# Conditioned encoder layer: the order of first loads and of first work, tiles of x against blocks of conditioning weights

## The chip, the core and the metric

The kernel runs on one core of a Trainium2 chip. The core has five engines with an instruction list each: TensorE (PE, matmuls; its weight loads are shown as PEld), VectorE (DVE), ScalarE (ACT), GpSimd (POOL) and SyncE (SP), which here only issues DMAs. Engines wait for one another by semaphores. The metric is the device time of one execution in microseconds (us).

## What is computed

One layer with a SwiGLU block, attention and a second SwiGLU block, each behind a normalisation that is scaled and shifted by a conditioning vector, on 1024 + 512 tokens of width 1024, in float32:

```python
def trunk(x, c):
    mod = jax.nn.silu(c) @ ada_w[l] + ada_b[l]          # (1024) x (1024, 9 * 1024)
    sh1, sc1, g1, sh2, sc2, g2, sh3, sc3, g3 = jnp.split(mod, N_MOD, axis=-1)
    h = modulate(rmsnorm(x, ffn1_norm[l]), sh1, sc1)    # h * (1 + scale) + shift
    x = x + 0.5 * g1[:, None, :] * swiglu(h, ffn1_wg[l], ffn1_wu[l], ffn1_wd[l])
    h = modulate(rmsnorm(x, mix_norm[l]), sh2, sc2)
    x = x + g2[:, None, :] * token_mixing(h, w_in[l], ...)
    h = modulate(rmsnorm(x, ffn2_norm[l]), sh3, sc3)
    x = x + 0.5 * g3[:, None, :] * swiglu(h, ffn2_wg[l], ffn2_wu[l], ffn2_wd[l])
    return rmsnorm(x, final_norm[l])
```

The first product needs x, turned so that its width lies along the partitions, the reciprocal root of each token's mean square, and the first two of the nine parts of `mod` (sh1 and sc1), which are the first 2048 columns of `ada_w`.

## The kernel before

All is in one program, `build`, in which each engine's list is written out: `start_loads` and `ffn_loads` for SP, `start_pe`, `start_act` and `start_dve` for the start, and then the first SwiGLU block (`ffn_*`), attention and the second SwiGLU block. The change touches the start, and in it the following.

**Tiles of x.** x has twelve tiles (`NT`) of 128 tokens and 512 KB each, four (`TPC`) to a chunk. They are loaded (L660) into `x_in`, a ring of four places; a place is loaded again when PE has transposed its tile (`x_turned`) and ACT has squared it (`x_summed`). For each tile ACT sums the squares (L767), PE makes eight transposes into PSUM (L671), and then DVE copies one half to `XT` (L853) and ACT the other (L770). Two pairs of PSUM banks take turns (`x_kept_v`, `x_kept_s`). After each chunk ACT takes a root (L774) and DVE makes reciprocals and four diagonal matrices (L859, L864), with which PE spreads the reciprocals over the partitions (L684) for ACT to copy (L780).

**Conditioning blocks.** `ada_w` comes in blocks of 512 columns, 2 MB each (L648). The first four, 0 to 3, give sh1 and sc1. ACT makes the high half of each weight (L800, four pieces for a block, into the ring `ada_hi`), DVE the low half (L806, four pieces), and PE multiplies the conditioning by both, 16 matmuls for a block (L714, L716, L719). ACT copies the result's row (`ada_keep`, L791) and PE turns it (`ada_turn`, L731). Blocks 4 and 5, for the gate, are multiplied as they are (L706, 32 matmul records).

**Order.** SP issues all twelve tiles of x and then the blocks, all in one queue. PE, ACT and DVE do the three chunks of x first, with the spreading in between, and then block after block. `ffn_loads` goes on with block 4, waits for the last tile of x to be transposed and squared, and loads the first weight quarters (`quart`, L2274), with block 5 among them.

**First product.** Behind the blocks DVE forms `mod` (L892, L896), multiplies x by its reciprocal roots (L2181, four times), and forms sums and low halves of the operands (L2209, L2221); ACT shifts and scales (L2192) and makes high halves (L2217). ACT and POOL make high and low halves of the weight units (L2383, L2389), and POOL sums of quarters (L2411). PE's products (L2852 to L2854, 24 matmuls each) take one unit and one operand after the other.

**Memory.** `ada_w_sb` fills the front of a region of which `HW` bytes per partition are used so. `x_in` lies directly behind it, where `ada_hi` lies afterwards, so that no high half can be made while x is there. `quart` lies 24576 bytes further on.

Of the kernel before, what the change touches and what calls it, by code (L numbers as in the profile page):

```python
# [13 lines left out]
F32 = mybir.dt.float32  # L14
# [6 lines left out]
P = 128  # L21
# [56 lines left out]
def build(nc, io):  # L78

    with ExitStack() as ctx:  # L80
# [39 lines left out]
        s1 = ExitStack()  # L120
        XR = 4
        x_in = sb(s1, "x_in", [P, XR, D])
        s1.close()
# [43 lines left out]
        rstd_p, rows = placed(HW + 57344, [("rstd_p", [P, 2, NB], F32), ("rows", [P, P], F32)])  # L167
        x_junk, diag = placed(HW + 40960, [("x_junk", [P, 2, D], F32), ("diag", [P, 2 * TPC, P], F32)])
# [218 lines left out]
        xt_parked, PARK0 = rows_landed, 16 * len(row_plan)  # L387
# [258 lines left out]
        def ada_block_load(sp, b):  # L646
            half, c = ada_home(b)
            sp.dma_start(ada_w_sb[:, half, :, c, :], ada_src[:, :, b * CH:(b + 1) * CH]).then_inc(ada_landed[b], 16)  # L648

        def start_loads(sp):  # L650
            sp.wait_ge(consts_set, 1)
            for src, r0, nr, w in row_plan:
                sp.dma_start(rows[r0:r0 + nr, 0:w], src).then_inc(rows_landed, 16)
            sp.dma_start(ident[:, :], io["ident"]).then_inc(consts_landed, 16)
            for t in range(NT):
                x, r = (io["x_prompt"], t * P) if t < S_PROMPT // P else (io["x_sample"], t * P - S_PROMPT)
                if t >= XR:
                    sp.wait_ge(x_turned, 2 + t - XR + 1)
                    sp.wait_ge(x_summed, t - XR + 1)
                sp.dma_start(x_in[:, t % XR, :], x[0, r:r + P, :]).then_inc(x_landed[t % XR], 16)  # L660
            for b in range(4):
                ada_block_load(sp, b)
# [73 lines left out]
        def start_pe(pe):  # L736
            pe.sem_inc(x_turned, 2)
            pe.sem_inc(sq_used, 2)
            pe.wait_ge(rows_landed, 16 * len(row_plan))
            pe.wait_ge(consts_landed, 16)  # L740
            pe.transpose(PS[:, 4, 0:NROW], rows[0:NROW, :], ident[0:NROW, 0:NROW]).then_inc(par_psum, 1)
            x_turn(pe, 0)
            x_turn(pe, 1)
            spread_pe(pe, 0)
            spread_pe(pe, 1)
            x_turn(pe, 2)
            pe.wait_ge(silu_ready, 2)
            ada_block(pe, 0)
            ada_block(pe, 1)
            ada_turn(pe, 0)  # L750
            for b in range(2, 6):
                ada_block(pe, b)
                if b < 4:
                    ada_turn(pe, b - 1)
                if b == 3:
                    ada_turn(pe, b)
            spread_pe(pe, 2)
            spread_pe(pe, 3)
            ada_turn(pe, 4)
            ada_turn(pe, 5)  # L760
# [32 lines left out]
        def ada_split_hi(act, b, p):  # L793
            half, c = ada_home(b)
            if p == 0:
                act.wait_ge(ada_landed[b], 16)
            if 4 * b + p >= AH // 2:
                act.wait_ge(ada_used, 4 * b + p + 1 - AH // 2)
# [10 lines left out]
        def start_act(act):  # L809
# [9 lines left out]
            x_sums(act, 0)  # L819
            x_sums(act, 1)  # L820
            spread_act(act, 0)
            spread_act(act, 1)
            x_sums(act, 2)
            for b in range(4):
                ada_split_hi(act, b, 0)
# [40 lines left out]
        def start_dve(dve):  # L866
# [12 lines left out]
            x_keep_dve(dve, 0)  # L879
            spread_dve(dve, 0)  # L880
            x_keep_dve(dve, 1)
            spread_dve(dve, 1)
            x_keep_dve(dve, 2)
            spread_dve(dve, 2)
            for b in range(4):
                for p in range(KD // 2):
# [2192 lines left out]
```

## Time and profile before

| | us |
|---|---|
| median of 3 runs | 2986.58 |
| lowest, highest | 2986.42, 2987.47 |
| profiled execution, its own time | 2986.62 |
| its span in the profile | 2984.8 |
| PE busy in the span | 2869.9 |
| POOL busy | 2231.1 |
| DVE busy | 1742.5 |
| ACT busy | 1553.8 |

The profile is of one execution. The busy share says how long an engine had an instruction in work; where an engine's row ends in square brackets, it had stood idle for so long before it, and the name behind the arrow is what released it. The granted clock of PE is given as a share of full speed. A timeline row that covers several instructions is marked x2, x8 and so on, and its length goes from the first one's start to the last one's end. Windows sum up a stretch of the execution.

### The profile page before, as it was taken

Reading aid. Unit: us, or ns where it says so; the run is one execution under the profiler, and the core shown is the slowest. Engines: PE = TensorE matmul, PEld = TensorE weight load, DVE = VectorE, ACT = ScalarE, POOL = GpSimd, SP = SyncE. Lnnn points to the kernel's source line nnn. Section 1 sums busy time; section 2 is a strip of 40 time slices with the busy share of each in tenths; the row PEclk is TensorE's granted clock in tenths of the full one; section 3 lists DMA queues with packets and bytes.
Section 4 is the critical chain, followed back from the end, with each engine's and each line's share of the span. In section 5 each row is a group of like instructions: output and inputs, shape, how many; then the busy total and the mean of one; then the engine's idle time right before and its main releaser. Section 6 shows DMA issues by size and latency. Waiting matters only on the chain. (4 is left out here: it accounts for less than half of the span.)

```text
span 2984.8 us, 49320 instructions
## 1 busy us (share of the span) xinstructions
PE 2869.9 (96%) x16057; PEld 2643.6 (89%) x16057; DVE 1742.5 (58%) x3002; ACT 1553.8 (52%) x2585; POOL 2231.1 (75%) x1116
## 2 busy tenths in 40 slices
PE   6899999999999999997999999999999999999998
PEld 3899999999999988885666667989999999999998
DVE  5666777767777657876543332274544467544545
ACT  6534444544444467766767775453444355444444
POOL 0788888889888853234557666678898888889884
PEclk9999999999999999998999999999999999999999
DMA  8333233333433335556322235441222232122224
GB/s 283 104 97 117 90 114 100 109 129 99 127 96 116 120 138 146 140 157 153 103 58 77 73 96 158 115 127 57 86 63 77 76 122 99 57 85 63 77 73 160
DMA packets 378610, 323.46 MB, mean 108 GB/s; under 512 B 22780, under 2 KB 325743, under 8 KB 378479
## 3 DMA queue, kind: packets, MB, share of 16 engines
q1 hardware_dynamic: 375342, 320.21, 35.4%
q10 hardware_dynamic: 3136, 1.57, 0.2%
q8 instruction: 74, 1.21, 0.2%
q14 instruction: 58, 0.47, 0.1%
HBM read 263.29 MB, written 58.43 MB: 108 GB/s over the span
## 5 line engine op out<-in xcount | busy, mean ns | idle before, releaser
L2389 POOL TENSOR_TENSOR W_lo<-quart,W_hi 128x1024 fp32r<-128x1024 f32 x384 | 941.8, 2471 | 178.4 <-ACT W_hi L2383 178.1
L2852 PE MATMUL PS<-SL,W_hi 128*128 128x384 f32 x2112 | 715.6, 339 | 31.7 <-issue 16.5
L2854 PE MATMUL PS<-SL,W_lo 128*128 128x384 f32 x2112 | 709.8, 336 | 0.0
L2853 PE MATMUL PS<-SL,W_hi 128*128 128x384 f32 x2112 | 709.7, 336 | 0.0
L2383 ACT ACTIVATE W_hi<-quart 128x1024 fp32r<-128x1024 f32 x384 | 402.9, 1060 | 561.8 <-PE PS L2918 245.0
L2054 DVE SCALAR_TENSOR_TENSOR XT<-PS,mod,XT 128x384 f32<-128x384 f32 (+1 forms) x840 | 418.4, 527 | 271.9 <-PE PS L2918 169.5
L2852 PEld LDWEIGHTS PS<-SL,W_hi 128*128 128x128 f32 x2112 | 399.3, 189 | 40.3 <-issue 24.0
L1844 POOL TENSOR_TENSOR XT_r<-XT,XT_r 128x512 fp32r<-128x512 f32 x224 | 286.9, 1286 | 179.0 <-ACT XT_r L1696 178.6
L2853 PEld LDWEIGHTS PS<-SL,W_hi 128*128 128x128 f32 x2112 | 399.3, 189 | 1.0 <-issue 1.0
L2854 PEld LDWEIGHTS PS<-SL,W_lo 128*128 128x128 f32 x2112 | 399.0, 189 | 0.0
L2411 POOL TENSOR_TENSOR quart<-quart 128x1024 f32<-128x1024 f32 x128 | 317.2, 2478 | 10.4 <-DVE qsum L2411 1.2
L2496 ACT ACTIVATE SLf<-PS 128x384 f32<-128x384 f32 x264 | 129.0, 491 | 290.0 <-PE PS L2854 289.9
L2684 DVE TENSOR_TENSOR PS<-PS,SLf 128x384 f32<-128x384 f32 x176 | 96.3, 562 | 236.4 <-ACT SLf L2496 224.2
L2411 POOL TENSOR_TENSOR qsum<-quart 128x1024 f32<-128x1024 f32 x63 | 151.1, 2398 | 105.0 <-DMA quart<-in_ffn_wu 75.2
L2918 PE MATMUL PS<-XT_r,W_lo 128*128 128x384 f32 x640 | 214.1, 334 | 0.0
L2917 PE MATMUL PS<-XT_r,W_hi 128*128 128x384 f32 x640 | 214.1, 334 | 0.0
L2916 PE MATMUL PS<-XT_r,W_hi 128*128 128x384 f32 x640 | 214.1, 334 | 0.0
L1752 DVE TENSOR_REDUCE mbuf<-PS 128x1 f32<-128x1024 f32 (+1 forms) x96 | 100.5, 1047 | 146.4 <-PE PS L1552 146.4
L1690 ACT ACTIVATE XT<-PS 128x512 f32<-128x512 f32 x224 | 133.1, 594 | 92.9 <-PE PS L1588 67.9
L2389 POOL TENSOR_TENSOR W_lo<-qsum,W_hi 128x1024 fp32r<-128x1024 f32 x64 | 159.8, 2496 | 4.2 <-ACT W_hi L2383 4.0
L2916 PE MATMUL PS<-hid,W_hi 128*128 128x384 f32 x480 | 160.8, 335 | 0.0
L2917 PE MATMUL PS<-hid,W_hi 128*128 128x384 f32 x480 | 160.5, 334 | 0.0
(314 smaller groups left out, 6385.9 us busy)
## 6 DMA issues: line engine op xcount, KB each, us to landing
quart<-in_ffn_wg SPq DMA_DIRECT2D x176, 256.0 KB, 3.1
quart<-in_ffn_wu SPq DMA_DIRECT2D x176, 256.0 KB, 3.4
quart<-in_ffn_wd SPq DMA_DIRECT2D x160, 256.0 KB, 3.0
ada_r<-in_ada_w SPq DMA_DIRECT2D x128, 192.0 KB, 2.5
raw<-in_w_out SPq DMA_DIRECT2D x30, 512.0 KB, 3.9
ada_w_sb<-in_ada_w SPq DMA_DIRECT2D x6, 2048.0 KB, 19.2
XT<-scr_xt SPq DMA_DIRECT2D x8, 1536.0 KB, 8.6
scr_xt<-XT SPq DMA_DIRECT2D x4, 2688.0 KB
```

The source lines that it names most:

```text
L1690: act.activation(e_slot(i), PS[:, 2 + i % 2, :], ACT.Exp).then_inc(exps_done, 1)
L1844: pool.tensor_tensor(p_lo(i), e_slot(i), p_hi(i).bitcast(F32), ALU.subtract).then_inc(p_lo_done, 1)
L2054: mm = dve.scalar_tensor_tensor(out=xt, in0=PS[:, bank, a - c * NB:b - c * NB], scalar=hgate[:, g, m, s:s + 1], in1=xt, op0=ALU.mult, op1= ...
L2383: act.activation(W_hi[:, slot_of(S, u), :], unit_src(u), ACT.Copy).then_inc(unit_hi, 1)
L2389: pool.tensor_tensor(W_lo[:, slot_of(S, u), :], unit_src(u), W_hi[:, slot_of(S, u), :].bitcast(F32), ALU.subtract) \
L2411: eng.tensor_tensor(flat(out), flat(a), flat(b), op).then_inc(sum_ready, 1)
L2852: pe.matmul(out, w_hi, m_hi, start=j in PRODUCT_OPENS and kp == 0, stop=False, skip_group_check=True)
L2853: pe.matmul(out, w_hi, m_lo, start=False, stop=False, skip_group_check=True)
L2854: mm = pe.matmul(out, w_lo, m_hi, start=False, stop=kp == 3, skip_group_check=True)
L2916: pe.matmul(out, w_hi, m_hi, start=n in PRODUCT_OPENS and kt == 0, stop=False, skip_group_check=True)
L2917: pe.matmul(out, w_hi, m_lo, start=False, stop=False, skip_group_check=True)
L2918: mm = pe.matmul(out, w_lo, m_hi, start=False, stop=kt == 1, skip_group_check=True)
```

## The change

`x_in` is placed where `quart` lies later. SP issues four tiles of x and block 0, four tiles and block 1, four tiles and block 2, and then block 3, in two DMAs of 1 MB with a semaphore each; ACT waits for the second ahead of its third piece. PE, ACT and DVE follow this order: ACT makes the high halves of block b behind the tiles of chunk b, DVE likewise the low halves, and PE multiplies block 0 ahead of chunk 1's transposes, and block 1 ahead of chunk 2's. No instruction of ACT, DVE or PE is added or taken away.

```diff
-        s1 = ExitStack()
         XR = 4
-        x_in = sb(s1, "x_in", [P, XR, D])
-        s1.close()
...
+        x_in, = placed(HW + 24576, [("x_in", [P, XR, D], F32)])
...
         def ada_block_load(sp, b):
             half, c = ada_home(b)
+            if b == 3:
+                for k, landed in ((0, ada_landed[3]), (KD // 2, ada_tail)):
+                    sp.dma_start(ada_w_sb[:, half, k:k + KD // 2, c, :], ada_src[:, k:k + KD // 2, b * CH:(b + 1) * CH])                       .then_inc(landed, 16)
+                return
...
-            for t in range(NT):
-                x, r = (io["x_prompt"], t * P) if t < S_PROMPT // P else (io["x_sample"], t * P - S_PROMPT)
-                if t >= XR:
-                    sp.wait_ge(x_turned, 2 + t - XR + 1)
-                    sp.wait_ge(x_summed, t - XR + 1)
-                sp.dma_start(x_in[:, t % XR, :], x[0, r:r + P, :]).then_inc(x_landed[t % XR], 16)
-            for b in range(4):
-                ada_block_load(sp, b)
+            for c in range(NCH):
+                for t in range(c * TPC, (c + 1) * TPC):
+                    x, r = (io["x_prompt"], t * P) if t < S_PROMPT // P else (io["x_sample"], t * P - S_PROMPT)
+                    if t >= XR:
+                        sp.wait_ge(x_turned, 2 + t - XR + 1)
+                        sp.wait_ge(x_summed, t - XR + 1)
+                    sp.dma_start(x_in[:, t % XR, :], x[0, r:r + P, :]).then_inc(x_landed[t % XR], 16)
+                ada_block_load(sp, c)
+            ada_block_load(sp, 3)
...
             x_turn(pe, 0)
+            pe.wait_ge(silu_ready, 2)
+            ada_block(pe, 0)
             x_turn(pe, 1)
             spread_pe(pe, 0)
             spread_pe(pe, 1)
-            x_turn(pe, 2)
-            pe.wait_ge(silu_ready, 2)
-            ada_block(pe, 0)
             ada_block(pe, 1)
             ada_turn(pe, 0)
+            x_turn(pe, 2)
...
+            if b == 3 and p == 2:
+                act.wait_ge(ada_tail, TAIL0 + 16)
...
-            x_sums(act, 0)
-            x_sums(act, 1)
-            spread_act(act, 0)
-            spread_act(act, 1)
-            x_sums(act, 2)
             for b in range(4):
+                if b < NCH:
+                    x_sums(act, b)
+                if b == 1:
+                    spread_act(act, 0)
+                    spread_act(act, 1)
                 ada_split_hi(act, b, 0)
                 ada_split_hi(act, b, 1)
...
-            x_keep_dve(dve, 0)
-            spread_dve(dve, 0)
-            x_keep_dve(dve, 1)
-            spread_dve(dve, 1)
-            x_keep_dve(dve, 2)
-            spread_dve(dve, 2)
             for b in range(4):
+                if b < NCH:
+                    x_keep_dve(dve, b)
+                    spread_dve(dve, b)
                 for p in range(KD // 2):
                     ada_split_lo(dve, b, p)
```

PE's list at its beginning, before: the transposes of x (from `x_in`), the spreading (`diag`), and then the matmuls of block 0 (`ada_hi`, `ada_w_r`).

```order
L741 MATMUL PS<-ident,rows 128x117
L671 MATMUL PS<-ident,x_in 128x128 x64
L684 MATMUL PS<-diag,ones 128x128 x6
L671 MATMUL PS<-ident,x_in 128x128 x32
L716 MATMUL PS<-ada_hi,c_hl 4x512
L719 MATMUL PS<-ada_w_r,c_hl 2x512
L714 MATMUL PS<-ada_w_r,c_hl 2x512
```

PE's list in the changed kernel, from the end of block 0 to the beginning of block 1. Line numbers are 4 higher here.

```order
L718 MATMUL PS<-ada_w_r,c_hl 2x512
L720 MATMUL PS<-ada_hi,c_hl 4x512
L675 MATMUL PS<-ident,x_in 128x128 x32
L688 MATMUL PS<-diag,ones 128x128 x6
L720 MATMUL PS<-ada_hi,c_hl 4x512
L723 MATMUL PS<-ada_w_r,c_hl 2x512
L718 MATMUL PS<-ada_w_r,c_hl 2x512
```

The 32 transposes of chunk 1 now stand between block 0 and the spreading, and block 1 behind that. The turn of the first row (`ada_row`) and the transposes of chunk 2 stand between block 1 and block 2:

```order
L718 MATMUL PS<-ada_w_r,c_hl 2x512
L720 MATMUL PS<-ada_hi,c_hl 4x512
L735 MATMUL PS<-fold,ada_row 128x2 x4
L675 MATMUL PS<-ident,x_in 128x128 x32
L720 MATMUL PS<-ada_hi,c_hl 4x512
L723 MATMUL PS<-ada_w_r,c_hl 2x512
L718 MATMUL PS<-ada_w_r,c_hl 2x512
```

ACT's list before, from the last tile of x over the last root to the high halves (L800) and the copies of rows (L791):

```order
L767 ACTIVATE x_junk,x_stat<-x_in 128x1024
L770 ACTIVATE XT<-PS 128x4x128
L774 ACTIVATE x_stat<-x_stat,eps_col 128x4
L800 ACTIVATE ada_hi<-ada_w_sb 128x1024 x6
L791 ACTIVATE ada_row<-PS 4x512
L800 ACTIVATE ada_hi<-ada_w_sb 128x1024 x4
L791 ACTIVATE ada_row<-PS 4x512
```

ACT's list in the changed kernel, from tile 7's copy to tile 8's:

```order
L774 ACTIVATE XT<-PS 128x4x128
L778 ACTIVATE x_stat<-x_stat,eps_col 128x4
L784 ACTIVATE rstd_p<-PS 128x384 x2
L806 ACTIVATE ada_hi<-ada_w_sb 128x1024 x2
L795 ACTIVATE ada_row<-PS 4x512
L806 ACTIVATE ada_hi<-ada_w_sb 128x1024 x2
L771 ACTIVATE x_junk,x_stat<-x_in 128x1024
L774 ACTIVATE XT<-PS 128x4x128
```

Block 1's four high halves and the copy of block 0's row stand between the chunks, where tile 8 followed the spreading's copies directly.

## Rows read from the trace of the kernel before

**Rows 1.** Page, part 1: busy us (share of span) and instructions, by engine
```profile
PE 2869.9 (96%) x16057; PEld 2643.6 (89%) x16057; DVE 1742.5 (58%) x3002; ACT 1553.8 (52%) x2585; POOL 2231.1 (75%) x1116
```

**Rows 2.** Windows: from:to length, busy us (count) of PE, PEld, DVE, ACT, POOL; clock, DMA
```profile
0.00:62.40 62.40, 38.08 (x207) 22.29 (x208) 30.73 (x51) 41.90 (x66) 0.94 (x5) 0.92 0.87 312
...
107.00:300.00 193.00, 191.65 (x1107) 189.40 (x1107) 123.39 (x229) 82.24 (x129) 167.83 (x71) 0.99 0.39 120
```

**Rows 3.** Windows of the start: PE clock, DMA share and GB/s stand last
```profile
7.00:14.00 7.00, 4.91 (x25) 4.19 (x25) 1.81 (x6) 4.23 (x9) 0.00 (x0) 1.00 0.95 354
...
14.00:21.00 7.00, 4.34 (x32) 3.42 (x32) 3.63 (x9) 6.97 (x14) 0.00 (x0) 1.00 0.77 266
...
21.00:28.00 7.00, 4.42 (x36) 4.02 (x36) 3.67 (x9) 6.04 (x14) 0.00 (x0) 1.00 0.82 260
...
36.50:42.00 5.50, 2.94 (x8) 0.86 (x8) 4.32 (x4) 3.89 (x4) 0.00 (x0) 0.50 1.04 387
```

**Rows 4.** Timeline, tiles of x: start us, length us, engine, line, operation, idle before
```profile
14.14 1.09 PE L671 MATMUL PS<-ident,x_in 128*128 128x128 f32 x8 [0.18 <-DMA x_in<-in_x_prompt]
...
22.08 0.59 ACT L770 ACTIVATE XT<-PS 128x512 f32<-128x512 f32 x1
...
23.59 0.59 ACT L770 ACTIVATE XT<-PS 128x512 f32<-128x512 f32 x1
...
24.07 0.30 ACT L774 ACTIVATE x_stat<-x_stat,eps_col 128x4 f32<-128x4 f32 x1
...
24.62 0.88 DVE L864 TENSOR_SCALAR diag<-ident,x_stat 128x128 f32<-128x128 f32 x4
...
26.10 1.05 ACT L767 ACTIVATE x_junk<-x_in 128x1024 f32<-128x1024 f32 x1
```

**Rows 5.** Timeline, last tile of x and first conditioning block
```profile
29.73 1.09 PE L671 MATMUL PS<-ident,x_in 128*128 128x128 f32 x8 [0.51 <-DMA x_in<-in_x_sample]
...
36.60 3.89 ACT L800 ACTIVATE ada_hi<-ada_w_sb 128x1024 fp32r<-128x1024 f32 x4 [4.12 <-DMA ada_w_sb<-in_ada_w]
...
37.69 4.63 DVE L806 TENSOR_TENSOR ada_w_r<-ada_w_sb,ada_hi 128x1024 fp32r<-128x1024 f32 x4 [4.08 <-ACT ada_hi L800]
...
39.06 0.58 PE L716 MATMUL PS<-ada_hi,c_hl 128*4 128x512 f32 x1 [8.23 <-DVE ada_w_r L806]
...
44.31 0.62 PE L716 MATMUL PS<-ada_hi,c_hl 128*4 128x512 f32 x2
```

**Rows 6.** Timeline, later conditioning blocks on PE, ACT and DVE
```profile
49.42 0.40 PE L716 MATMUL PS<-ada_hi,c_hl 128*4 128x512 f32 x1
...
50.73 0.40 PE L716 MATMUL PS<-ada_hi,c_hl 128*4 128x512 f32 x1
...
54.96 0.59 ACT L791 ACTIVATE ada_row<-PS 4x512 f32<-4x512 f32 x1
...
55.45 1.99 ACT L800 ACTIVATE ada_hi<-ada_w_sb 128x1024 fp32r<-128x1024 f32 x2
...
56.53 2.36 DVE L806 TENSOR_TENSOR ada_w_r<-ada_w_sb,ada_hi 128x1024 fp32r<-128x1024 f32 x2 [0.21 <-ACT ada_hi L800]
```

**Rows 7.** Timeline, operand preparation and first products on DVE, POOL and PE
```profile
64.23 6.76 DVE L2181 TENSOR_TENSOR SLf<-XT,rstd_p 128x1536 f32<-128x1536 f32 x4
...
70.83 2.40 POOL L2411 TENSOR_TENSOR qsum<-quart 128x1024 f32<-128x1024 f32 x1 [6.81 <-DMA quart<-in_ffn_wu]
...
71.02 3.82 DVE L2209 TENSOR_TENSOR SLf<-SLf 128x1536 f32<-128x1536 f32 x1
...
90.30 0.66 PE L2852 MATMUL PS<-SL,W_hi 128*128 128x384 f32 x1 [7.06 <-issue]
...
91.79 1.75 DVE L2209 TENSOR_TENSOR SLf<-SLf 128x1536 f32<-128x1536 f32 x1
...
107.01 0.45 PE L2852 MATMUL PS<-SL,W_hi 128*128 128x384 f32 x1 [2.18 <-POOL W_lo L2389]
...
108.41 0.52 PE L2852 MATMUL PS<-SL,W_hi 128*128 128x384 f32 x1
```

More of the change, by code:

```diff
@@ L386, in build @@
         raw_kept, RAW0, t_made, MADE0 = diag_ready, NT, x_inv, NCH
-        xt_parked, PARK0 = rows_landed, 16 * len(row_plan)
+        ada_tail, TAIL0 = rows_landed, 16 * len(row_plan)
+        xt_parked, PARK0 = rows_landed, TAIL0 + 16
         xt_unparked, BACK0 = [consts_landed, ada_landed[5]], 16
```

## The prediction

> **What bounds the kernel now.** I read the page's busy shares first, then the windows of the start against a stretch of the body, then the timeline of the first 110 us, engine by engine. TensorE is busy for 2869.9 of 2984.8 us [rows 1]. In the body nothing is left to win: 191.65 of 193.00 us busy between 107 and 300 us. The start is different: 38.08 of the first 62.40 us, most of it transposes and thin matmuls that wait for data [rows 2]. The change edits the start alone. All its waits are relative (a semaphore of another engine), nothing later stands at a fixed time, and the body is bound by PE, so what the start gains or loses reaches the end undiminished. The question is when DVE has done its last low half of a conditioning block (57.7 to 58.89 in the profiled run) [rows 6], for the modulation, the operands of the first product and its matmuls follow from that.
>
> Two things hold up the start now. While x is loaded, the DMA engines move 260 to 266 GB/s, against 387 afterwards [rows 3], because the ring of four tiles is refilled only as ACT and PE release it. Then ACT stands for 4.12 us before block 0, 6.9 us after the last tile of x had landed (29.7 to 36.6), and DVE and PE for as long [rows 5]. From there the blocks come in every 5.4 us, as fast as the queue moves 2.1 MB at 387 GB/s, and the engines follow them.
>
> **The transfers.** The change fills the holes in the queue: 14 us at about 263 instead of 387 GB/s are 14 x (1 - 263/387) = 4.5 us of transfer time. With block 0 behind four tiles, the queue has moved 2.48 MB by 14 us [rows 3] (some 0.15 before 7 us), and tiles, rows and block 0 are 4.3 MB, so its data are over at 14 + 1.7/0.387 = 18.4 us. Bounds of the landing: tile 3 landed at 14.14 [rows 4], plus 5.4 us of one block, 19.5; or plus the 6.9 us that block 0 took behind the last tile before [rows 5], 21.0. I take 20.3, in the middle, ACT beginning at 20.4. After that no data are late: tiles 4 to 7 and block 1 are 4.2 MB, 10.8 us, down at about 31; tiles 8 to 11 are released until 34 and are down by 39, block 3 some 11 us later; each is wanted later than that, as follows. The new half loads of block 3 and the wait on their second half (ACT, before its third piece) therefore cost nothing; uncovered, they would cost at most a half block, 2.7 us. The ring's new place costs nothing either: SP already waited for all tiles before it loaded the first weight quarter, though this wait now ends at about 51 us, with the queue still busy on block 4.
>
> **The engines.** Each engine runs its list in order, and the lists are now woven: four tiles, one block. The work is the same, instruction for instruction. What is new is who stands behind whom: the copies of tile 4 on ACT wait for PE's transposes, which stand behind block 0's 16 matmuls, which wait for DVE's low halves, which wait for ACT's high halves. This round trip through four engines comes twice more. I lay it out with offsets from rows.
>
> Block 0. ACT begins at 20.4. In the trace the first matmul came 2.46 us after ACT's begin (36.60, 39.06), and the next thing on PE could start 7.94 us after it (the second matmul of the row at 44.31 starts at 44.54) [rows 5]. PE was at half clock for the first 3.9 us of these (0.50 granted between 36.5 and 42.0 [rows 3]), after standing 8.23 us; in the new order it stands from 15.2 to 22.9, as long, so I keep the offset. Tile 4's transposes start at 28.3 and its copy on ACT at 29.4. ACT had finished the four high halves at 24.4 and one square at 25.4: it stands for 4.0 us. From then on a tile takes 1.51 us (22.08 to 23.59), the square root comes 0.48 after the fourth copy, and ACT is free 2.03 after the root's begin (24.07, 26.10) [rows 4]. So 29.4 + 3 x 1.51 + 0.48 + 2.03 = 36.5.
>
> Block 1. High halves from 36.5, at 0.95 us each (four in 3.89 [rows 5]) with one 0.49 copy of the row between; done at 40.8, and tile 8's square after it. DVE's fourth low half ends at 42.3. PE starts at 39.0, after 3 us of idling; a gap of 2.18 us in the trace (107.01) was followed by matmuls at half clock (0.52 us instead of 0.33, 108.41) [rows 7], so I take half clock for as long as in block 0: nine matmuls at 0.425 and seven at 0.23, the last starting at 44.2. At full clock PE would follow DVE and be done 1.1 earlier. Then comes the turn of the row, 1.31 us from last matmul to what follows (49.42, 50.73) [rows 6]. Tile 8 is transposed from 45.5 and copied from 46.6; ACT stands for 4.7 us. Three more tiles and the root: 46.6 + 4.53 + 0.48 = 51.6.
>
> Blocks 2 and 3. ACT goes on at 51.8, but DVE first makes the diagonals, until 1.43 after the root's begin (24.07; 24.62 and 0.88 [rows 4]), so its low halves start at 53.1. PE, idle since about 50, starts at 54.5 and, at half clock again, ends block 2 at 60.1 (5.65 from the first matmul to the end of the last, 39.06 to 44.71 [rows 5]); if DVE set its pace, at 58.9, 1.2 earlier. ACT's copy of that row waits for it, then come the last two high halves. From this copy to the end of DVE's last low half passed 3.93 us (54.96, 55.45, then 56.53 and 2.36 to 58.89) [rows 6]: 60.1 + 3.93 = 64.0, against 58.89. The start is 5.2 us longer.
>
> **Behind it.** The quarters' data land at about 66, before they are wanted; now they are late and POOL stands 6.81 us for them (70.83) [rows 7]. That is no gain. DVE and POOL delay one another: beside POOL's sum one DVE operation of 1.75 us takes 3.82 (71.02; alone 91.79), 2.1 us for each POOL operation. Now five such fall between DVE's row at 64.23 and its end at 93.5: three sums and two low halves: four and seven DVE operations, 6.76 + 12.0, and 5 x 2.1 make 29.3 us, as seen. With the data there, the three sums move ahead beside the four L2181, which alone took 6.76; the number of overlapped operations stays five. The first product starts about 2 us later within this stretch, but PE stands 7.06 us before the second anyway (90.30) [rows 7]. What changes is ACT's shift of block B22, which now ends 16.9 us after DVE's first L2181, while DVE could go on after 16.5: 0.4 us. Bounds: 0 (all absorbed in later waits on POOL, 2.18 at 107.01) and 2.1 (one more collision). I take 0.4.
>
> **Sum.** The profiled execution took 2986.62, that is its span 2984.8 and 1.8 around it; the median of the runs is 2986.58, the same. 2986.6 + 5.2 + 0.4 = 2992.2 us, 0.19% more.
>
> **Rivals.** (1) PE keeps its clock, or has it back sooner, in blocks 1 and 2: less 1.1 and 1.2, 2989.9 us. For it speaks that the pauses are shorter (3 and 4.5 us) than the two of 8.23 and 7.06 us behind which half clock was certain; against it the row at 108.41, behind 2.18 us. (2) Slower by more than can be argued away: the three sums beside L2181 cost one further collision that DVE pays. It comes about if POOL's low half of the third unit, until now over by 88.6, slips behind DVE's T1 and T3 operations, since ACT, now delayed by 3 to 4 us in this stretch, makes its high half later; its place is 20 to 29 us after the first L2181, and it decides as soon as DVE's last L2209 ends over 1 us later than the start's shift. Price 2.1: 2994.3 us, +0.26%. (3) Faster: the transfers were the bound and the engines hide their waits in one another. Then the last block is worked on as it lands, about 5 us earlier, 2981.6 us; at the best ACT's own work behind block 0's landing, 30.9 us (16 high halves, 8 tiles, three rows, roots), gives 51 instead of 57.4, 2980.2. Against it: PE's list forces the round trip, and DVE cannot lower a half that ACT hasn't made.
>
> The Trainium skill, DMA: Bandwidth & Descriptors, section Rules for kernel authors, advises to issue a DMA early, compute, and wait on its semaphore late. By that rule alone the third rival would hold; the 4.12 us that ACT waits for block 0 agree that there is time to hide, and no row shows the woven order. The Trainium skill, SBUF — State Buffer, section SBUF: two separate sides, says that such a pair of VectorE and GpSimd operations excludes one another for a whole instruction. By it a collision would cost DVE up to POOL's 2.4 us rather than 2.1, and the second rival would be 2994.6.
>
> **How the numbers follow.** Forecast 0.50, rival 1 0.22, rival 2 0.22, rival 3 0.06. A measurement can tell about 0.2% here, 6.0 us: above 2992.55 is slower, below 2980.6 faster. The forecast's own range is 2990.7 to 2993.7 (landing of block 0 between 19.5 and 21.0, the tail between 0 and 1), a third of it above the bound; with nearly all of rival 2: slower 0.37. Rival 3 reaches the lower bound in its best half: faster 0.03. The rest, 0.60, is the same. The range goes from rival 1 with the early landing and nothing behind it, and a little clock saved in block 0 (2988.7 - 1.2 = 2987.5), to rival 2 with the late landing, 2995.3.
>
> **What would show it.** Right: DMA above 340 GB/s from 7 to 28 us; ACT standing about 4 us before tile 4's copy and 4 to 5 before tile 8's, with PE as releaser; half clock in blocks 1 and 2; the last low half ending near 64; the sums on POOL without a wait for DMA; a body as before. Wrong: waits for blocks or tiles behind block 0, the last low half before 60, or a second product that starts over 2 us off the shift of the start.

## The result, and the profile after

| | before | changed |
|---|---|---|
| median of 20 runs each, us | 2987.99 | 2993.28 |
| lowest, highest | 2982.95, 2995.27 | 2985.39, 2997.81 |
| profiled execution, its own time | 2986.62 | 2994.61 |
| its span | 2984.8 | 2992.8 |

The ratio is 1.0015, with a 95% interval of 1.0008 to 1.0022: 4.5 us more, 2.4 to 6.6. (The medians themselves differ by 5.3 us; I go by the ratio.) The forecast was 2992.2, 0.19% more. The interval contains it, and most of it lies below the 0.2% that I had taken as the bound of "slower".

The windows of the start, by the columns of [rows 3], in the changed kernel:

```profile
7.00:14.00 7.00, 4.91 (x24) 4.66 (x25) 1.81 (x5) 3.96 (x9) 0.00 (x0) 1.00 0.97 374
14.00:21.00 7.00, 1.23 (x12) 0.99 (x10) 3.56 (x8) 6.66 (x11) 0.00 (x0) 0.96 1.04 401
21.00:28.00 7.00, 6.75 (x32) 3.37 (x33) 4.20 (x5) 3.51 (x6) 0.00 (x0) 0.79 1.03 392
```

The holes in the transfers are filled, as meant: 401 and 392 GB/s where [rows 3] had 266 and 260. What ACT waited for between 8 and 66 us, before and then changed (total, times, longest):

```profile
ACT ada_hi L800 <- DMA ada_w_sb<-in_ada_w: 6.4, 4, 4.1
ACT ada_row L791 <- PE PS L716: 3.8, 3, 2.6
...
ACT XT L770 <- PE PS L671: 0.9, 1, 0.9
```

```profile
ACT XT L774 <- PE PS L675: 9.2, 3, 4.8
ACT ada_row L795 <- PE PS L720: 5.4, 2, 2.8
...
ACT ada_hi L806 <- DMA ada_w_sb<-in_ada_w: 0.3, 1, 0.3
```

6.1 us of waiting for blocks are gone, and 9.9 us of waiting for PE have come (8.3 for the copies of x, 1.6 for the rows). The timeline of ACT shows where (copies of x are L774, high halves L806, copies of rows L795):

```profile
18.79 3.90 ACT L806 ACTIVATE ada_hi<-ada_w_sb 128x1024 fp32r<-128x1024 f32 x4 [0.31 <-DMA ada_w_sb<-in_ada_w]
...
27.22 0.60 ACT L774 ACTIVATE XT<-PS 128x512 f32<-128x512 f32 x1 [3.49 <-PE PS L675]
...
44.51 0.60 ACT L774 ACTIVATE XT<-PS 128x512 f32<-128x512 f32 x1 [4.82 <-PE PS L675]
...
49.55 0.31 ACT L778 ACTIVATE x_stat<-x_stat,eps_col 128x4 f32<-128x4 f32 x1
...
58.78 0.59 ACT L795 ACTIVATE ada_row<-PS 4x512 f32<-4x512 f32 x1 [2.79 <-PE PS L720]
```

The same on PE, where blocks 0, 1 and 2 (L720) begin behind a pause and at half clock, that is, at the lower of the two levels of the granted clock (1.2 instead of 2.4 GHz): the first matmul takes 0.59 us instead of 0.40. The rows at 40.88 and 57.77 are the first that are shorter again; in block 0 that is the one at 23.77.

```profile
21.25 0.59 PE L720 MATMUL PS<-ada_hi,c_hl 128*4 128x512 f32 x1 [6.02 <-DVE ada_w_r L812]
26.14 2.93 PE L675 MATMUL PS<-ident,x_in 128*128 128x128 f32 x24
...
36.65 0.59 PE L720 MATMUL PS<-ada_hi,c_hl 128*4 128x512 f32 x1 [2.78 <-DVE ada_w_r L812]
...
40.88 0.43 PE L718 MATMUL PS<-ada_w_r,c_hl 128*2 128x512 f32 x1
...
52.26 0.59 PE L720 MATMUL PS<-ada_hi,c_hl 128*4 128x512 f32 x1 [4.42 <-ACT ada_row L795]
...
57.77 0.52 PE L720 MATMUL PS<-ada_hi,c_hl 128*4 128x512 f32 x1
```

And on DVE, the end of the low halves (L812), the modulation (L895, L899), the four multiplications of x (L2184), and the third operand's first operation (L2212 at 94.14):

```profile
50.90 6.92 DVE L812 TENSOR_TENSOR ada_w_r<-ada_w_sb,ada_hi 128x1024 fp32r<-128x1024 f32 x6
60.35 2.36 DVE L812 TENSOR_TENSOR ada_w_r<-ada_w_sb,ada_hi 128x1024 fp32r<-128x1024 f32 x2 [2.53 <-ACT ada_hi L806]
66.26 0.34 DVE L895 TENSOR_TENSOR mod<-PS,par 128x16 f32<-128x16 f32 x3 [3.55 <-PE PS L735]
66.63 3.54 DVE L899 SCALAR_TENSOR_TENSOR mod<-mod,par 128x8 f32<-128x8 f32 x3
70.21 11.09 DVE L2184 TENSOR_TENSOR SLf<-XT,rstd_p 128x1536 f32<-128x1536 f32 x4
...
85.08 1.76 DVE L2212 TENSOR_TENSOR SLf<-SLf 128x1536 f32<-128x1536 f32 x1 [0.44 <-ACT SLf L2195]
...
94.14 3.95 DVE L2212 TENSOR_TENSOR SLf<-SLf 128x1536 f32<-128x1536 f32 x1
```

The last low half ends at 62.71, 3.8 us after the 58.89 of [rows 6]. Further on I follow two marks on POOL, before and then changed: the first sum of the next weight quarters, and the low half behind it:

```profile
113.28 2.39 POOL L2411 TENSOR_TENSOR qsum<-quart 128x1024 f32<-128x1024 f32 x1 [1.64 <-DMA quart<-in_ffn_wu]
...
131.16 2.40 POOL L2389 TENSOR_TENSOR W_lo<-quart,W_hi 128x1024 fp32r<-128x1024 f32 x1 [1.17 <-ACT W_hi L2383]
```

```profile
117.77 2.39 POOL L2414 TENSOR_TENSOR qsum<-quart 128x1024 f32<-128x1024 f32 x1 [1.65 <-DMA quart<-in_ffn_wu]
...
135.65 2.40 POOL L2392 TENSOR_TENSOR W_lo<-quart,W_hi 128x1024 fp32r<-128x1024 f32 x1 [1.18 <-ACT W_hi L2386]
```

Both are 4.49 us later, which is the 4.5 us of the ratio. The profiled execution's own difference, 8.0 us, has another 3.5 us somewhere in the body, which no run here explains. The runs of either kernel spread over 12 us, and a second profiled execution of the changed kernel (below) had a span of 2985.9, so I explain the 4.5 and not the 8.0.

### The profile page after: what moved, and what is told of

Same layout as the page of the kernel before. It is cut to its first block and busy times, and to the rows that moved or that the text cites. A ratio compares the mean times of both kernels' runs of the same rounds, so it can differ in the third digit from the quotient of the medians.

```text
span 2992.8 us, 49322 instructions
## 1 busy us (share of the span) xinstructions
PE 2874.7 (96%) x16057; PEld 2644.9 (88%) x16057; DVE 1740.2 (58%) x3002; ACT 1552.8 (52%) x2585; POOL 2232.8 (75%) x1116
## 5 line engine op out<-in xcount | busy, mean ns | idle before, releaser
L2855 PE MATMUL PS<-SL,W_hi 128*128 128x384 f32 x2112 | 716.4, 339 | 26.8 <-POOL W_lo L2392 15.7
L2919 PE MATMUL PS<-hid,W_hi 128*128 128x384 f32 x480 | 160.7, 335 | 0.2 <-POOL W_lo L2392 0.2
L2921 PE MATMUL PS<-hid,W_lo 128*128 128x384 f32 x480 | 160.4, 334 | 0.0
```

The costliest lines, as they stand in the source:

```text
L2855: pe.matmul(out, w_hi, m_hi, start=j in PRODUCT_OPENS and kp == 0, stop=False, skip_group_check=True)
L2919: pe.matmul(out, w_hi, m_hi, start=n in PRODUCT_OPENS and kt == 0, stop=False, skip_group_check=True)
L2921: mm = pe.matmul(out, w_lo, m_hi, start=False, stop=kt == 1, skip_group_check=True)
```

## The experiments

All kernels share two parts of the story, so the marks of all of them stand in one table: the end of DVE's last low half, the beginning of the modulation (L892 before), and the two marks on POOL. All are us in the profiled execution; the ratio is against the kernel before, with its interval.

| kernel | last low half | modulation | mark 1 | mark 2 | ratio |
|---|---|---|---|---|---|
| before | 58.89 | 62.43 | 113.28 | 131.16 | |
| changed | 62.71 | 66.26 | 117.77 | 135.65 | 1.0015 [1.0008, 1.0022] |
| ring_only | 59.14 | 62.69 | 113.50 | 131.41 | 0.9999 [0.9989, 1.0008] |
| loads_only | 60.49 | 64.03 | 115.52 | 131.09 | 1.0005 [0.9996, 1.0015] |
| two_ahead | 55.29 | 58.83 | 109.72 | 127.62 | 0.9980 [0.9972, 0.9989] |
| warm | 58.91 | 62.46 | 113.49 | 131.81 | 1.0005 [0.9996, 1.0014] |
| sums_late | 63.08 | 66.62 | 117.53 | 133.19 | one run, 2988.91 us |
| row_late | 54.45 | 59.23 | 110.09 | 128.01 | one run, 2985.78 us |
| row_late_warm | 56.48 | 60.24 | 111.10 | 129.00 | 0.9982 [0.9973, 0.9991] |
| weave_full | 52.68 | 56.45 | 107.41 | 122.88 | 0.9979 [0.9970, 0.9988] |
| changed_again | 62.96 | 66.50 | 118.09 | 133.62 | 1.0007 [0.9998, 1.0016] |

**The loads alone.** The changed kernel's loads, with the engines' lists of before:

```diff
             x_turn(pe, 0)
-            pe.wait_ge(silu_ready, 2)
-            ada_block(pe, 0)
             x_turn(pe, 1)
             spread_pe(pe, 0)
             spread_pe(pe, 1)
+            x_turn(pe, 2)
+            pe.wait_ge(silu_ready, 2)
+            ada_block(pe, 0)
             ada_block(pe, 1)
             ada_turn(pe, 0)
-            x_turn(pe, 2)
```

ACT's and DVE's lists likewise.

> The changed kernel with its loads (four tiles, one block) and the ring's place, but with the engines' lists as before: all of x first, then the blocks. If the round trip through the four engines is what costs (theory), then this order has none: ACT meets tiles 8 to 11 late, at 31 to 35 us, ends x at about 37 and then makes all sixteen high halves without waiting for data; DVE's last low half ends at 38.1 + 16 x 1.145 = 56.5 us, against 58.9 before and 62.7 in the changed kernel; the whole is 1.7 us (0.06%) faster than before. If the order of the loads itself costs (rival), the last low half ends after 60 us here too.

The low halves ended at 60.49, later than before instead of earlier: my theory's number failed, and by the bound that I had set (60 us) the order of the loads does cost, 1.6 us with these lists. On ACT's timeline there are two reasons. The chunks of x now stand behind blocks in the queue, and then the row copies wait for PE once a block:

```profile
20.54 1.06 ACT L771 ACTIVATE x_junk<-x_in 128x1024 f32<-128x1024 f32 x1 [2.09 <-DMA x_in<-in_x_prompt]
...
31.11 1.06 ACT L771 ACTIVATE x_junk<-x_in 128x1024 f32<-128x1024 f32 x1 [1.18 <-DMA x_in<-in_x_sample]
...
46.35 0.59 ACT L795 ACTIVATE ada_row<-PS 4x512 f32<-4x512 f32 x1 [2.19 <-PE PS L720]
51.45 0.59 ACT L795 ACTIVATE ada_row<-PS 4x512 f32<-4x512 f32 x1 [0.73 <-PE PS L720]
56.57 0.59 ACT L795 ACTIVATE ada_row<-PS 4x512 f32<-4x512 f32 x1 [0.73 <-PE PS L720]
```

The rows of ACT come 5.10 and 5.12 us apart although all data are there: this is the pace of the loop of high half, low half, matmuls and row copy. In the kernel before they come as far apart, at 44.74, 49.86 and 54.96 [rows 6]:

```profile
44.74 0.59 ACT L791 ACTIVATE ada_row<-PS 4x512 f32<-4x512 f32 x1 [0.73 <-PE PS L716]
...
49.86 0.59 ACT L791 ACTIVATE ada_row<-PS 4x512 f32<-4x512 f32 x1 [0.41 <-PE PS L716]
```

The waits for data among them are 0.21 and 0.52 us, and the 1.52 us that ACT waited for block 1 were followed by these 0.73 us of waiting for PE. So from the first row copy on the blocks already ran at the loop's pace, and earlier data could shorten only the wait ahead of block 0 (4.12 us). The order of the loads by itself gives more than that away again: x on ACT is done at 38.18 and not at 32.16, and the high halves begin at 38.37 and not at 36.60.

**The ring's place alone.** Only `x_in` is moved, in the kernel before:

```diff
-        s1 = ExitStack()
         XR = 4
-        x_in = sb(s1, "x_in", [P, XR, D])
-        s1.close()
...
+        x_in, = placed(HW + 24576, [("x_in", [P, XR, D], F32)])
```

> The kernel before with nothing changed but the place of the ring of x, which moves to the weight quarters' place. Theory: nothing waits for it, the last low half ends at 58.9 us and the first weight quarter is issued as before; 0.0% within the measurement. Rival (the place matters, since the first quarter's load has to wait for the ring): the quarters land later, and the first products start later by as much.

All marks are within 0.26 us of before and the ratio is 0.9999. The place costs nothing, as the prediction had it.

**The round trip taken out.** PE transposes two tiles of the next chunk before it goes into a block, so that ACT has something to copy; row 0 is turned behind chunk 2:

```diff
-        def x_turn(pe, c):
-            for t in range(c * TPC, (c + 1) * TPC):
+        def x_turn(pe, c, tiles=range(TPC)):
+            for t in (c * TPC + i for i in tiles):
...
+            x_turn(pe, 1, (0, 1))
             pe.wait_ge(silu_ready, 2)
             ada_block(pe, 0)
-            x_turn(pe, 1)
+            x_turn(pe, 1, (2, 3))
             spread_pe(pe, 0)
             spread_pe(pe, 1)
+            x_turn(pe, 2, (0, 1))
             ada_block(pe, 1)
+            x_turn(pe, 2, (2, 3))
             ada_turn(pe, 0)
-            x_turn(pe, 2)
```

> The changed kernel, but PE transposes the first two tiles of a chunk ahead of the block that stands before that chunk (two pairs of PSUM banks are free for them), and turns the first row behind the third chunk. Theory: ACT no longer stands before the copies of tile 4 (3.5 us in the changed kernel) and tile 8 (4.8 us), at most 1 and 2 us before tiles 6 and 10; the last low half ends at about 56 us, not 62.7, and the whole is about 2.5 us (0.1%) faster than before and 6 to 7 faster than the changed kernel. Rival (DVE or the transfers set the pace in the woven order): the last low half stays within 2 us of 62.7.

ACT's waits of over 1.3 us up to 52 us:

```profile
28.02 0.60 ACT L776 ACTIVATE XT<-PS 128x512 f32<-128x512 f32 x1 [1.38 <-PE PS L675]
...
51.36 0.59 ACT L797 ACTIVATE ada_row<-PS 4x512 f32<-4x512 f32 x1 [2.54 <-PE PS L720]
```

The waits of 3.49 and 4.82 us before chunk 1 and chunk 2 have become 1.38 and none. The modulation begins 7.4 us earlier than in the changed kernel and 3.6 earlier than before, and the kernel is faster than the one before by 0.2%. Loads, work and memory are the changed kernel's; only the place of 32 transposes and one turn in PE's list is another. This shows that the order in PE's list, with its round trip, is what makes the changed kernel slower. The new order also takes away PE's pause ahead of block 1, so this run doesn't tell how much of the 7.4 us is the clock; the next one does.

**The clock's part.** The changed kernel, with matmuls of ones ahead of blocks 0, 1 and 2, which nobody reads and which keep PE busy through its pauses:

```diff
+        def keep_warm(pe, bank, n):
+            for _ in range(n):
+                pe.matmul(PS[:, bank, 0:P], ones[:, :], ones[:, :], start=True, stop=True)
...
+            keep_warm(pe, 6, 20)
             pe.wait_ge(silu_ready, 2)
             ada_block(pe, 0)
...
+            keep_warm(pe, 4, 10)
             ada_block(pe, 1)
...
+                if b == 2:
+                    keep_warm(pe, 7, 16)
```

> The changed kernel with matmuls of ones on ones, whose results nobody reads, in PE's pauses ahead of the blocks: 20 ahead of block 0, 10 ahead of block 1, 16 ahead of block 2. Theory (PE's half clock after its pauses is part of the round trip): the blocks' matmuls start at 0.23 us one after the other instead of 0.43; block 0 is over 0.5 us sooner, block 1 1.0 sooner than that, ACT's copy of block 2's row comes 2.0 sooner than that; the last low half ends at 59.2 us instead of 62.7, and ACT still stands over 2.5 us before tile 4's copy and over 3 before tile 8's. Rival (the pauses and the order alone cost, the clock nothing, since DVE sets the pace): within 1 us of 62.7.

PE's blocks now begin at full clock (0.39 and 0.40 us a matmul), and ACT's waits are shorter, but still there:

```profile
26.72 0.60 ACT L782 ACTIVATE XT<-PS 128x512 f32<-128x512 f32 x1 [2.83 <-PE PS L675]
...
42.78 0.60 ACT L782 ACTIVATE XT<-PS 128x512 f32<-128x512 f32 x1 [3.58 <-PE PS L675]
...
54.99 0.59 ACT L803 ACTIVATE ada_row<-PS 4x512 f32<-4x512 f32 x1 [0.72 <-PE PS L720]
```

DVE's last eight low halves begin at 49.16, and block 2 on PE behind them:

```profile
49.16 6.92 DVE L820 TENSOR_TENSOR ada_w_r<-ada_w_sb,ada_hi 128x1024 fp32r<-128x1024 f32 x6
...
50.53 0.40 PE L720 MATMUL PS<-ada_hi,c_hl 128*4 128x512 f32 x1 [0.85 <-ACT ada_row L803]
```

3.49, 4.82 and 2.79 us have become 2.83, 3.58 and 0.72. The modulation begins at 62.46, 3.8 us earlier than in the changed kernel and as in the one before. The half clock thus costs 3.8 us, and with a full clock the woven order is no slower and no faster than the old one; the ratio of 1.0005 fits that, though its interval overlaps with that of the changed kernel. The order costs more than the clock: in weave_full (below), where all blocks run at full clock too, the modulation begins at 56.45, another 6.0 us earlier, some 0.4 of it for another place of the row's copy.

**POOL's sums held back.** In the changed kernel the three sums of quarters wait until DVE has done its four L2184:

```diff
+                pool.wait_ge(op_x, OPX0 + 4)
```

> The changed kernel, but POOL waits with its three sums until DVE has done its four L2184, as they came about before when the quarters landed late. Theory: the sums cost the first product 2 us or more, but the stretch behind it nearly nothing: DVE's first L2212 behind the sums starts earlier, the first product 2 to 5 us earlier, and DVE's operation for T3 (the last L2212) ends 0.7 us earlier against its row at the start of L2184, as in the kernel before. Rival (the number of collisions is what counts and it changes): more than 2 us either way at T3.

L899 is short again, and so are the four L2184 (6.77 us); the long operations come later (L2224 at 76.90 takes 3.92 us):

```profile
66.62 0.34 DVE L895 TENSOR_TENSOR mod<-PS,par 128x16 f32<-128x16 f32 x3 [3.54 <-PE PS L735]
67.00 1.39 DVE L899 SCALAR_TENSOR_TENSOR mod<-mod,par 128x8 f32<-128x8 f32 x3
...
96.12 1.75 DVE L2212 TENSOR_TENSOR SLf<-SLf 128x1536 f32<-128x1536 f32 x1
```

From the modulation's beginning to the end of the third operand's first operation the changed kernel took 31.83 us (66.26 to 98.09), this one 31.25 (66.62 to 97.87). To mark 1 it is 51.51 against 50.91. The first product starts at 82.69 instead of 86.09. So 0.6 of the 0.7 us that the changed kernel loses behind the start come from POOL's early sums; the other collisions only change places.

Mark 2 moved by more. From mark 1 to mark 2 the changed kernel took 17.88 us, this one 15.66. The windows from 100 to 120 us, of the changed kernel and of this one, differ in the granted clock (third number from the end):

```profile
110.00:115.00 5.00, 3.50 (x14) 3.50 (x15) 0.56 (x1) 1.70 (x4) 5.00 (x3) 0.76 0.53 155
115.00:120.00 5.00, 5.00 (x28) 5.00 (x27) 1.52 (x5) 1.17 (x3) 3.35 (x2) 0.89 0.91 273
```

```profile
110.00:115.00 5.00, 3.69 (x21) 3.69 (x22) 0.56 (x1) 1.84 (x3) 5.00 (x3) 1.00 0.50 146
115.00:120.00 5.00, 5.00 (x31) 5.00 (x30) 2.86 (x9) 2.24 (x5) 3.40 (x2) 1.00 0.91 279
```

PE stood about as long just before in both (3.26 us up to 111.50, 3.24 up to 111.31), and fell to half clock in the one and not in the other. By the table, the way from mark 1 to mark 2 has two lengths in all eleven executions, 17.9 (18.3 in warm) or 15.5 to 15.7 us. In changed_again the clock fell earlier, behind the pause up to 104.07 (0.71 granted from 105 to 110 us), and the next pause was shorter (1.66 us): there a fall costs nothing, behind the last pause it costs 2.2 to 2.4 us. Nothing in the changed kernel's lists decides it, since its two executions show one each.

**The row's copy behind the high halves.** To two_ahead is added that ACT copies the row of a block after all four high halves of the next, not between the second and the third:

```diff
-                if b > 0:
-                    ada_keep(act, b - 1)
                 ada_split_hi(act, b, 2)
                 ada_split_hi(act, b, 3)
+                if b > 0:
+                    ada_keep(act, b - 1)
```

> The kernel two_ahead, with ACT's copy of a block's row placed behind all four high halves of the next block instead of between the second and the third. Theory (PE's half clock in block 2 sets the pace there, not the place of the copy): DVE's last low half ends 2 us earlier (53 instead of 55.3), but PE's last matmul of block 3 at most 0.5 earlier than at 56.4, and DVE's first modulation operation at most 0.5 before 58.8. Rival (the copy's place alone holds block 3 up): that operation comes 2 us earlier.

DVE now runs through its last eight low halves without a wait, and ends them at 54.45, 0.8 earlier than two_ahead, but the modulation comes 0.4 later:

```profile
45.28 9.17 DVE L814 TENSOR_TENSOR ada_w_r<-ada_w_sb,ada_hi 128x1024 fp32r<-128x1024 f32 x8
59.23 0.34 DVE L897 TENSOR_TENSOR mod<-PS,par 128x16 f32<-128x16 f32 x3 [4.78 <-PE PS L735]
```

Block 2 was again at half clock behind a pause of 3.44 us, and so was block 0 from 23.50 to 26.20, which in two_ahead had been at full clock; tile 6 then waited 2.75 us instead of 1.38. Measured from the start of the eight low halves, the modulation comes after 13.95 us instead of 15.13 (58.83 less 43.70). Not all of these 1.2 us are the edit's: in block 2 eight matmuls were slow and not twelve, each by 0.2 us. With all blocks at full clock the same stretch takes 13.30 us with the old place of the copy (warm, 49.16 to 62.46) and 12.93 with the new one (the next two runs), so the copy's place itself is worth some 0.4 us.

**The row's copy and the clock.** The same with dummy matmuls, of which I put the first eight behind tile 5's transposes and not ahead of tile 4's:

```diff
             x_turn(pe, 1, (0, 1))
+            keep_warm(pe, 6, 8)
             pe.wait_ge(silu_ready, 2)
             ada_block(pe, 0)
...
+                if b == 2:
+                    keep_warm(pe, 7, 11)
```

> The kernel row_late with matmuls of ones in PE's pauses, 8 ahead of tile 4 and 11 ahead of block 2. Theory: now block 2 follows DVE's low halves, and the first modulation operation comes at about 56.5 us, 2.3 earlier than in two_ahead; the whole is 2 us faster than two_ahead, about 0.25% faster than before. Rival: as in row_late, no more than 0.5 us.

The modulation began at 60.24, not at 56.5. The dummies stood behind tile 5's transposes, thus behind its data, and only delayed block 0; tile 6 waited for 4.07 us. Block 2 was at full clock, and from the start of the low halves (47.31) it took 12.93 us, 1.0 less than in row_late. The place of the first dummies was my error, and half of the experiment is lost by it.

**All of it.** The first dummies right behind chunk 0, where PE pauses:

```diff
             x_turn(pe, 0)
+            keep_warm(pe, 6, 16)
+            x_turn(pe, 1, (0, 1))
             pe.wait_ge(silu_ready, 2)
             ada_block(pe, 0)
...
+                if b == 2:
+                    keep_warm(pe, 7, 11)
```

> The changed kernel with all that the runs point to: PE takes two tiles ahead of each block, ACT copies a row behind the next block's four high halves, and matmuls of ones fill PE's pauses ahead of tile 4 (16) and ahead of block 2 (11). In row_late_warm the first filling stood behind tile 5 instead, and held block 0 up by 2.5 us. Theory: block 0's matmuls start as soon as its first low half is done or tile 5 is transposed (about 22), all blocks run at full clock, the diagonals of chunk 2 are done at about 43.5, and the first modulation operation comes 12.9 us behind that, at 56.5 us, against 62.4 before and 58.8 in two_ahead; the whole is about 6 us (0.2%) faster than before, not distinguishable from two_ahead within the measurement. Rival: the pauses move elsewhere, and the modulation comes after 58 us.

PE's timeline has no pause of over 1.3 us from 16 to 60 us, and the blocks begin at 22.48, 35.32 and 44.88, none at half clock (the transposes between 32.2 and 35.3 are):

```profile
15.65 3.74 PE L742 MATMUL PS<-ones 128*128 128x128 f32 x32
20.35 1.09 PE L675 MATMUL PS<-ident,x_in 128*128 128x128 f32 x8 [0.97 <-DMA x_in<-in_x_prompt]
...
44.88 0.40 PE L720 MATMUL PS<-ada_hi,c_hl 128*4 128x512 f32 x1 [0.24 <-DVE ada_w_r L821]
```

The modulation began at 56.45, 6.0 us earlier than before and 9.8 earlier than in the changed kernel, where 56.5 was expected. The median of 11 runs is 2981.69 us against 2988.45 of the kernel before on the same chip; the ratio is 0.9979, 6.3 us less. It is faster than both kernels, but by its ratio not to be told from two_ahead (0.9980), though its modulation begins 2.4 us earlier.

**The changed kernel again.** The same file on another chip, beside weave_full:

> The changed kernel itself, on the chip and beside the runs of weave_full. Theory: the start is as in its first profile within 0.5 us (first modulation operation at 66.3, the low half of the sixth unit pair at 135.7 us), and the 3.5 us by which its first profiled execution was longer than the start explains don't come back in the ratio: 0.15% (4.5 us) slower than before. Rival (something behind the start is slower in the changed kernel): the ratio is 0.25% or more, and the profiled spans differ by 8 us again.

The modulation began at 66.50 and mark 1 at 118.09, 4.8 us later than before. Mark 2 is at 133.62, only 2.5 later, since this execution was at full clock from 110 to 120 us. Inside the start the two executions of the same kernel differ more than at its end: here PE was slow for 4.2, 5.1 and 2.5 us in blocks 0, 1 and 2, and in the first one for 2.5, 4.2 and 5.5. ACT's copies of tiles 4 and 8 came at 28.27 and 46.05 instead of 27.22 and 44.51, and the two modulations are 0.24 us apart all the same. The ratio, 1.0007, has an interval that ends at 1.0016, so it doesn't speak for my 1.0025 rival; it overlaps with the first one between 1.0008 and 1.0016. By the two together the change costs some 2.4 to 4.8 us, and whether it is nearer to the one or the other may hang on how often the clock falls behind 105 us in either kernel, which a profile of one execution doesn't tell.

## Why the prediction was right, point by point

**The transfers: right, and 1.5 us too late.** I took block 0's landing at 20.3, between 19.5 and 21.0. ACT began at 18.79, before the early bound. The sum that I had worked out myself at 387 GB/s (18.4) was the right one, as the windows show 374 and 401; I had not trusted it, and had taken the middle of two ends that came from the slower queue of before. No data were late after that, as said: the 0.31 us before block 0 are ACT's only wait for a block, so the halved load of block 3 cost nothing.

**What bounds the start: half right.** ACT's wait of 4.12 us for block 0 was real, and the later blocks did come in every 5.4 us. That this sets the engines' pace was wrong: their own loop takes 5.1 us a block (loads_only), and from the first row copy on they ran at that. It did not enter the sum, but it was the ground on which rival 3 stood.

**The round trip: right in place and size.** ACT stood 3.49 us before tile 4's copy (4.0 predicted) and 4.82 before tile 8's (4.7), both released by PE. From ACT's beginning to PE's next work it was 7.35 us and not the 7.94 taken over from [rows 5], since half clock ended earlier in block 0 of this execution. From tile 4's copy to tile 8's 17.29 us passed; I had 17.2. With these two, the last root is at 49.55 and not at 51.6.

**The half clock: right, and too small.** I had it for as long as in the kernel before (3.9 us). It lasted 2.5 us in block 0, 4.2 in block 1 and 5.5 in block 2, and in the second execution otherwise. The way from block 2's first matmul to ACT's copy of the row was therefore 6.52 us (52.26 to 58.78), where I had put 5.6 (54.5 to 60.1). 0.9 of the 2.2 us won by then are lost again there. Rival 1, full clock in blocks 1 and 2, priced at 2.3 us, did not come: both began at half clock. Its price was too low: the run with the dummies puts all three blocks at 3.8. Stretch by stretch it is 0.7 in block 0, which the price left out, 1.2 in block 1 (1.1 predicted) and 2.1 in block 2 (1.2 predicted), less 0.2 by which ACT began later in that run.

**The start as a whole.** 5.2 us predicted (by its own terms 64.0 less 58.89, 5.1), 3.8 measured. The terms that were mis-sized are the landing of block 0 (1.6 us too much) and the price of the half clock (0.6 too much in block 0, 0.9 too little in block 2).

**Behind the start.** 0.4 us predicted (0 to 2.1), 0.7 measured. DVE's wait for ACT's shift came in its place (0.44 before the L2212 at 85.08), the three sums ran without a wait for data (67.81), and, besides a low half that meets L899 in both kernels, five operations of POOL delayed DVE, as many as before. But they weren't the five I had named: one of the sums met not L2184 but the small L899, which took 3.54 us instead of the 1.39 that it takes in sums_late. POOL's rows show it:

```profile
65.50 2.34 POOL L2392 TENSOR_TENSOR W_lo<-quart,W_hi 128x1024 fp32r<-128x1024 f32 x1 [65.03 <-ACT W_hi L2386]
67.81 2.34 POOL L2414 TENSOR_TENSOR qsum<-quart 128x1024 f32<-128x1024 f32 x1
```

L899 ends at 70.17, with the sum. Its first operation alone takes 1.24 us in both kernels and ends with POOL's low half (at 67.84 here, at 64.02 before), so that even the 1.39 us are mostly a wait. In the three executions where that happened (changed, changed_again, loads_only) the way from the modulation to mark 1 is 51.5 to 51.6 us, and in the eight others 50.8 to 51.0. The number of collisions doesn't explain this, but ACT's shifts do: they begin behind L899 and the first L2184, and so 2.15 us late, and DVE meets the last of them. In warm, where all three sums met the multiplications of x, as I had assumed, the shift had ended 0.7 us before DVE wanted it (80.05 against 80.76). So the way by which I came to 0.4 us didn't occur, and that its size was nearly right is luck. The Trainium skill, SBUF — State Buffer, section SBUF: two separate sides, says that the loser of such a pair waits for the other's whole instruction. The trace agrees: L899 took 2.15 us more beside a POOL operation of 2.34, and both of its waits end with POOL's operation, within 0.03 us. PE's pause of 7.06 us before the second product [rows 7], which I had named as the cover for a later first product, is gone: the first product began at 86.09 and ran at half clock until 92.0, and the second followed it at once (93.15, 2.9 us later than before, within the 2 us of the start's shift that I had named). Rival 2, one more collision, did not come.

**Rival 3, transfers bound.** The transfers did come earlier, and it did not help: with loads_only, where the engines' lists are not woven, the low halves ended 1.6 us later than before. The Trainium skill, DMA: Bandwidth & Descriptors, section Rules for kernel authors, has the issue early and the wait late; here it held for the waits (6.4 us on DMA became 0.3) and not for the time, because in a list that runs in order the work on the early data stands ahead of other work. In weave_full, with the same loads, the gain does come, 6 us, near to what rival 3 had as its best case.

**The sum.** 5.6 us predicted, 4.5 measured: 3.8 + 0.7. That the ratio agrees with it is in part luck, as the clock between 105 and 120 us moves an execution by 2.3 us, half of the effect. The forecast's own range also had a slip: with its bounds for the landing and the tail it goes from 2991.0 to 2993.5 and not from 2990.7 to 2993.7.

## What to carry to other kernels

Before weaving two chains of work into lists that run in order, follow one item round all engines: where the first instruction of the next item stands behind the last of the present one on any engine, the round trip is paid once an item, however early the data come. Give each engine one or two items of the other chain ahead of its wait, and look at what the pauses do to TensorE's clock, as they can cost over half as much as the order does (here 3.8 against 6.0 us). And find the pace of the loop behind a transfer before speeding the transfer up: here it was 5.1 us a block, and the transfers' 5.4, so that only the wait ahead of the first block was to be won.

## What the runs showed of the hardware

- Half clock came behind a pause of 2.78 us and lasted for 4.2 us, and behind one of 4.42 us and lasted for 5.5 us; behind the longest of the changed kernel, 6.02 us, it lasted for 2.5 us only. In the kernel's second execution pauses of 6.73, 2.79 and 4.43 us were followed by 4.2, 5.1 and 2.5 us of it. It need not begin with the work: in loads_only PE stood for 4.37 us, did three matmuls at 0.40 us, and then eight (from 41.58 on) took about 0.6. The length of the pause does not give the length of the slow stretch.
- At the same place of PE's list, behind pauses of 3.24 to 3.26 us, PE fell to half clock in changed, warm and row_late_warm and not in sums_late; and the changed kernel itself fell there in one execution and one product earlier, behind 2.54 us, in the other. 2.2 to 2.4 us hang on it. A part of the spread of 12 us between runs of one kernel may be that; this was not measured.
- The order of requests in one queue was also the order of landing at the start: four tiles and a block of 2 MB landed by 18.8 us, when the engines moved 374 to 401 GB/s, and tile 4, requested behind the block, at 20.5 (loads_only, where ACT waited for it).
- Operations of DVE on 8 columns were delayed by POOL as much as those on 1536: the three of L899 took 3.54 us beside a low half and a sum on POOL, and 1.39 beside the low half alone. One sum costs them 2.15 us, and DVE's operations on 1536 columns 2.0 to 2.2.
